# A two-block transformer on one core: query projections cut into pieces between the sums of a gather, and a triangular inverse with 64-column stationaries

## The reference, cut to what matters

```python
def peer(h, w_pq, sub_keys, expert_u, expert_v):       # 2 blocks of 128 tokens
    q = (xb @ w_pq).reshape(128, 8, 2, 128)            # w_pq 1024 x 2048
    s = jnp.einsum('thpd,hpkd->thpk', q, sub_keys)     # scores against 128 keys, twice
    sv, si = lax.top_k(s, 16)
    ...
    best, pos = lax.top_k(cand, 16)                    # 16 experts for each of 8 heads
    g = jax.nn.softmax(best, axis=-1)
    act = jax.nn.gelu(jnp.einsum('thkd,td->thk', expert_u[eidx], xb))
    return jnp.einsum('thk,thkd->td', g * act, expert_v[eidx])
```

```python
    A = jnp.where(strict, jnp.einsum('bhnik,bhnjk->bhnij', kb, k) * decay, 0.0)
    T = lax.linalg.triangular_solve(A + eye, eye, left_side=True, lower=True, unit_diagonal=True)
    u = jnp.einsum('bhnij,bhnjv->bhniv', T, v * beta[..., None])
```

## Time and profile before

| | |
|---|---|
| time, median of 3 (lowest, highest) | 1871.20 us (1868.68, 1879.18) |
| profiled execution, its own time | 1862.66 us |
| its span, mean granted TensorE clock | 1860.9 us, 0.915 |
| PE, DVE, ACT, POOL busy | 85%, 51%, 28%, 31% |
| DMA | 438.5 MB, 236 GB/s over the span |
| the gathers' queue | 299.86 MB |
| picks' stage | about 250 to 1001 us |
| inverse | about 1146 to 1172 and 1566 to 1593 us |

### The profile page before, as it was taken

How to read it: one execution, slowest core, us unless ns; L and a number is a source line. 1 busy time by engine, 2 the same in 40 slices (tenths; PEclk the granted TensorE clock), 3 DMA queues, 4 the chain that set the end, 5 groups by cost and what they waited for, 6 DMA issues and landing times.

```text
span 1860.9 us, 18421 instructions
## 1 busy us (share of the span) xinstructions
PE 1572.5 (85%) x5974; PEld 966.6 (52%) x5974; DVE 955.0 (51%) x2207; ACT 527.7 (28%) x1470; POOL 580.8 (31%) x596
## 2 busy tenths in 40 slices
PE   7998988886758667546646999999999999999998
PEld 2644654343434223212212587677775587677775
DVE  1786666756666666678876346421123246421122
ACT  2244323432223324222322254321112244321111
POOL 0010056655565767677764002100000002100000
PEclk9999999987878788767767999999999999999999
DMA  9864089988897999999999532175442422175410
GB/s 364 317 237 176 1 330 360 364 321 316 328 373 285 379 347 379 354 374 400 398 366 402 180 112 70 49 251 166 158 147 99 150 101 81 39 250 174 159 46 23
DMA packets 170725, 438.50 MB, mean 236 GB/s; under 512 B 12531, under 2 KB 59027, under 8 KB 170500
## 3 DMA queue, kind: packets, MB, share of 16 engines
q0 software_dynamic: 81824, 299.86, 42.7%
q1 hardware_dynamic: 88806, 137.46, 21.2%
HBM read 436.23 MB, written 1.05 MB: 235 GB/s over the span
## 4 chain that ended last, share of the span: by engine, by line
PE 64%; issue 11%; DVE 8%; POOL 8%; ACT 2%; DMA 2%; DVEq 2%; another core or an unknown queue 1%; SPq 0%; ACTq 0%; POOLq 0%
PE psum L1192 15%; PE psum L1203 6%; PE psum L836 5%; PE psum L966 4%; PE psum L837 4%; POOL arena L1339 4%; POOL arena L1334 4%; PE psum L668 4%; DVE arena L2296 3%; PE psum L874 2%; PE psum L1217 2%; PE psum L1180 2%; PE psum L648 2%; PE psum L850 1%; PE psum L992 1%
## 5 line engine op out<-in xcount | busy, mean ns | idle before, releaser
L836 PE MATMUL psum<-arena 128*128 128x512 f32 x382 | 249.5, 740 | 204.7 <-issue 106.6
L2296 DVE CUSTOM_DVE_ANT_0 arena<-arena,psum 128x1024 f32<-128x1024 f32 x224 | 273.6, 1221 | 185.8 <-DMA arena<-in_expert_u,indices 117.8
L1339 POOL DMA_INDIRECT arena<-in_expert_v,indices x256 | 252.8, 988 | 163.0 <-issue 71.8
L1334 POOL DMA_INDIRECT arena<-in_expert_u,indices x256 | 250.6, 979 | 92.8 <-issue 71.2
L1192 PE MATMUL psum<-activations_T,weight_ring 128*128 128x256 f32 x1280 | 279.2, 379 | 0.0
L1192 PEld LDWEIGHTS psum<-activations_T,weight_ring 128*128 128x128 f32 x1280 | 243.0, 190 | 39.8 <-issue 7.6
L836 PEld LDWEIGHTS psum<-arena 128*128 128x128 f32 x382 | 76.9, 226 | 337.3 <-issue 207.3
L2538 DVE SCALAR_TENSOR_TENSOR arena<-psum,small,arena 128x254 f32<-128x254 f32 (+1 forms) x176 | 76.8, 478 | 321.1 <-ACT arena L1797 317.5
L837 PE MATMUL psum<-arena 128*128 128x512 f32 x382 | 231.7, 693 | 0.0
L1288 POOL TENSOR_TENSOR small<-small 128x1 f32<-128x1 f32 (+5 forms) x30 | 30.7, 1024 | 532.6 <-DVE small L2432 194.4
L1614 ACT ACTIVATE activations_T<-activations_T 128x1 f32<-128x1 f32 x256 | 51.1, 200 | 348.0 <-DVE activations_T L2296 185.0
(11 more groups left out here) (408 smaller groups left out, 2052.3 us busy)
## 6 DMA issues: line engine op xcount, KB each, us to landing
weight_ring<-in_ffn_w_in SPq DMA_DIRECT2D x44, 1024.0 KB, 7.8
weight_ring<-in_w_in SPq DMA_DIRECT2D x14, 2048.0 KB, 8.4
arena<-in_ffn_w_out POOLq DMA_DIRECT2D x22, 1024.0 KB, 5.3
weight_ring<-in_w_ada SPq DMA_DIRECT2D x8, 2048.0 KB, 11.5
weight_ring<-in_w_out SPq DMA_DIRECT2D x6, 2048.0 KB, 8.5
weight_ring<-in_w_ada SPq DMA_DIRECT2D x16, 512.0 KB, 9.5
weight_ring<-in_w_pq SPq DMA_DIRECT2D x4, 2048.0 KB, 19.3
weight_ring<-in_w_in SPq DMA_DIRECT2D x2, 2080.0 KB, 21.7
```

The lines of the kernel that those rows point to most:

```text
L836: mm(o0, DIAG[:, j % ND, :], VROWS[n % NV][:, 0:512], start=m == 0, stop=last)
L1334: nc.gpsimd.indirect_dma_start(UROWS[g % NU], None, a["expert_u"], bass.IndirectOffsetOnAxis(ap=where, axis=0)).then_inc(sem(f"u_row{g % N ...
L1339: nc.gpsimd.indirect_dma_start(VROWS[g % NV], None, a["expert_v"], bass.IndirectOffsetOnAxis(ap=where, axis=0)).then_inc(sem(f"v_row{g % N ...
L2296: ttr(out=DOTJ[n >= UNIT], in0=UROWS[n % NU], in1=h2, scale=1.0, scalar=0.0, op0=ALU.mult, op1=ALU.add, accum_out=DOT[:, i, m:m + 1]).then ...
```

## The change

`queries` becomes a generator that pauses after every four matmuls (8 passes). The table runs one piece ahead of each of eight successive picks: block (0,2) before picks 13 to 20, (0,3) before 35 to 42, (1,0), (1,1), (1,2) before 53 to 60, 69 to 76, 85 to 92; (1,3) goes by two pieces before picks 101 to 104; (0,1) stays whole at pick 1. Scores, adds and the other engines' order in this stage stay.

In the inverse L1068 and L1080 take a stationary of 64 columns for each of the two sides, whose outputs go to partitions 0 to 63 and 64 to 127, and a moving operand of 64 columns; TW becomes 64 wide, its copies 256 columns, and VectorE subtracts the two diagonal blocks by an instruction each.

```diff
@@ -263,7 +263,8 @@
         RTMP = v(C0 + 2048, 2, 512)
         TI = v(C0, 8, P)
         TU = v(C0 + 1024, 8, P)
-        TW = v(C0 + 2048, 8, P)
+        TW = v(C0 + 2048, 8, 64)
+        SIDES = [slice(0, 64), slice(64, P)]
         QKT2 = v(C0 + 3072, 2, 4, SEQ)
         MO1 = v(0, 2, D, of=XT)
         AM = v(C0 + 3072, 2, 8, P)
@@ -666,10 +667,14 @@
                 for f in range(4):
                     for k in range(KT):
                         ins = mm(o[:, f * P:(f + 1) * P], wpq[b][:, k, f * P:(f + 1) * P], H2T[i][:, k, :], start=k == 0, stop=k == KT - 1)
-                ins.then_inc(a_full, 1)
-                if i == 1:
-                    was_read("a", 3 - b)
-                at["pqt"][i, b] = c["a"]
+                        if k == 3:
+                            yield
+                    if f == 3:
+                        ins.then_inc(a_full, 1)
+                        if i == 1:
+                            was_read("a", 3 - b)
+                        at["pqt"][i, b] = c["a"]
+                    yield
 
             def first_queries(hh):
                 if hh == 0:
@@ -784,11 +789,13 @@
             output(outputs[0], 1, 0, 4, KT).then_inc(d_full, 1)
             output(outputs[1], 1, 1, 4, KT).then_inc(d_full, 3)
             last_read[ON_PE[at["wout"] + 1]] = ("d", at["out1"])
-            coming = {1: lambda: queries(0, 1), 6: lambda: scores(0, 1), 20: lambda: queries(0, 2), 27: lambda: scores(0, 2),
-                      34: lambda: h2_turned(1), 42: lambda: queries(0, 3), 50: lambda: scores(0, 3),
+            coming = {6: lambda: scores(0, 1), 27: lambda: scores(0, 2), 34: lambda: h2_turned(1), 50: lambda: scores(0, 3),
                       PICKS - 12: lambda: h2_back(1, bank_a, a_full)}
+            for i, b, last, count in [(0, 1, 1, 1), (0, 2, 20, 8), (0, 3, 42, 8)] + [(1, b, QAT[b], 8 if b < 3 else 4) for b in range(4)]:
+                pieces = queries(i, b)
+                for n in range(last - count + 1, last + 1):
+                    coming[n] = lambda pieces=pieces, count=count: [next(pieces) for _ in range(8 // count)]
             for b in range(4):
-                coming[QAT[b]] = lambda b=b: queries(1, b)
                 coming[QAT[b] + 8] = lambda b=b: scores(1, b)
 
             def transposed(m, i, count):
@@ -1065,7 +1072,8 @@
                         if lv == 6:
                             ins = mm(o[64:P, h * 64:(h + 1) * 64], AT[0:64, half, h, 64:P], TI[0:64, n, 0:64], start=True, stop=True)
                             continue
-                        ins = mm(o[:, h * P:(h + 1) * P], AM[:, lv % 2, n, :], TI[:, n, :], start=True, stop=True)
+                        for side in SIDES:
+                            ins = mm(o[side, h * 64:(h + 1) * 64], AM[:, lv % 2, n, side], TI[:, n, side], start=True, stop=True)
                     ins.then_inc(a_full, 1)
                     tw[half] = c["a"]
 
@@ -1077,7 +1085,8 @@
                         o = bank_d()
                         for h in range(DH):
                             n = half * 4 + h
-                            ins = mm(o[:, h * P:(h + 1) * P], TU[:, n, :], TW[:, n, :], start=True, stop=True)
+                            for side in SIDES:
+                                ins = mm(o[side, h * 64:(h + 1) * 64], TU[:, n, side], TW[:, n, :], start=True, stop=True)
                         ins.then_inc(d_full, 1)
                         t_done[half] = c["d"]
                     m["level"].append(c["d"])
@@ -1093,7 +1102,7 @@
                     o = bank_d()
                     for h in range(DH):
                         n = half * 4 + h
-                        ins = mm(o[0:64, h * 64:(h + 1) * 64], TW[64:P, n, 0:64], TU[64:P, n, 64:P], start=True, stop=True)
+                        ins = mm(o[0:64, h * 64:(h + 1) * 64], TW[64:P, n, :], TU[64:P, n, 64:P], start=True, stop=True)
                     ins.then_inc(d_full, 1)
 
                 pe.wait_ge(d_free, c["d"])
@@ -1730,21 +1739,22 @@
                     o = full()
                     act.copy(BROWS[:, i, :, :], o.rearrange("p (h j) -> p h j", h=4)).then_inc(a_free, 1)
                 af(Z2[:, :, :], Z2[:, :, :], ACT.Silu).then_inc(sem("z_silu"), 1)
-                def heads_of(T, half):
+
+                def heads_of(T, half, width):
 
                     o = full()
-                    act.copy(T[:, 4 * half:4 * half + 4, :], o.rearrange("p (h j) -> p h j", h=4)).then_inc(a_free, 1)
+                    act.copy(T[:, 4 * half:4 * half + 4, :], o[:, 0:4 * width].rearrange("p (h j) -> p h j", h=4)).then_inc(a_free, 1)
 
                 for half in range(2):
-                    heads_of(TW, half)
+                    heads_of(TW, half, 64)
                 for lv in range(1, 6):
                     for half in range(2):
-                        heads_of(TU, half)
+                        heads_of(TU, half, P)
                         if lv < 5:
-                            heads_of(TW, half)
+                            heads_of(TW, half, 64)
                         else:
                             o = full()
-                            act.copy(TW[64:P, 4 * half:4 * half + 4, 0:64], o[64:P, 0:256].rearrange("p (h j) -> p h j", h=4)).then_inc(a_free, 1)
+                            act.copy(TW[64:P, 4 * half:4 * half + 4, :], o[64:P, 0:256].rearrange("p (h j) -> p h j", h=4)).then_inc(a_free, 1)
                 for i in range(2):
                     o = full()
                     squares([(v(C0 + 3072 + (4 * i + h) * P, P), o[:, h * P:(h + 1) * P], i * 4 + h) for h in range(DH)])
@@ -2476,7 +2486,10 @@
                             continue
                         o = full()
                         if lv < 6:
-                            tt(TI[:, s, :], TI[:, s, :], o.rearrange("p (h j) -> p h j", h=4), ALU.subtract).then_inc(d_free, 1)
+                            for side in SIDES:
+                                diagonal = TI[side, s, side]
+                                ins = tt(diagonal, diagonal, o[side, 0:256].rearrange("p (h j) -> p h j", h=4), ALU.subtract)
+                            ins.then_inc(d_free, 1)
                         else:
                             corner = TU[0:64, s, 64:P]
                             tt(corner, corner, o[0:64, 0:256].rearrange("p (h j) -> p h j", h=4), ALU.subtract).then_inc(d_free, 1)
```

## The result

| | before | changed |
|---|---|---|
| median of 4 runs (lowest, highest) | 1872.72 us (1868.68, 1879.18) | 1846.20 us (1838.72, 1850.80) |
| profiled execution, its span | 1862.66, 1860.9 us | 1838.72, 1836.9 us |
| first projection behind the gather begins at | 1019.0 us | 999.4 us |

The ratio is 0.9867, with a 95% interval of 0.9835 to 0.9899: 25 us less, where the forecast was 28. That held in the run groups in which the kernel before takes 1865 to 1873 us. The record names the chip of each later group: those with 1865 ran on two chips (5 and 8), both groups with 1775 and 1776 on a third (3). Whether the chip itself makes the difference is not shown: these are three chips, and the hour changed with them.

The account below looks back on a forecast made before the run. The gather stage was taken as bound by its gathers, with time lost where TensorE's starved query blocks delay sums. -22 and -6 make -28: 1834.7 us profiled, 1843 as median, range 1823 to 1868.

Parts of the forecast that it names:

- -22 for the pieces: Gather stage: query blocks split ahead of picks' sums remove most GpSimd waits; -22 us, at best -38.1.
- -6 for the inverse: Inverse: two column groups side by side cut a level from 4.55 to 3.7 us; -6 us, bounds -9 and +6.
- The waits go: Gather stage: GpSimd's five waits for picks' sums, 38.1 us in all, shrink to 0 to 5 us each.
- The pace behind them: Stretch of the five blocks: without waits, 3.18 us a pick falls to the later stretch's 2.81, worth 28.9 us.
- The model with one stock and one rate: TensorE in the windows: prefetched instructions plus steady supply; (0,3) and (1,1) dry up, about 7 us of 28.9 left.
- cease to arrive: TensorE in query blocks: instructions stop coming after 44 to 46 passes while gathers saturate the DMA; (1,0) takes 23.0 us.
- the one that I had put second: Dried-up windows: a sum stands within 8 passes, not at the block's end; waits of 4 to 5 us, not 8 to 9.
- There the stage is bound by the gathers: Gather stage from 640.8 us on, no query blocks: 2.81 us a pick, read as the DMA's limit.
- The multiply: Inverse: L2469, 2.64 us on VectorE between two subtractions, stops being wholly covered; 0.4 us a layer.
- The rival of serial groups: Inverse: column groups run one after another, a level takes 5.2 us, +5 in eight; 1854 us, chance 0.12.
- cold windows: TensorE's windows stay at the lower clock level, waits of 7 us remain, only the inverse gains; 1862 to 1866, chance 0.15.
- slower: Gather stage: missing instructions now hit the sums too, +35 us less 6; about 1900 us, chance 0.11.

Follow-up runs that it names:

- pieces_only: The changed kernel with the old inverse, so only the query blocks in pieces of 8 passes: 1843.75 us, ratio 0.9873 to the kernel before.
- half_rows: The kernel before, whole blocks, with most gathers fetching 2 KB a row instead of 4: 1872.4 us in a single run.
- groups_in_turn: The changed kernel with the inverse's matmuls four of one column group, then four of the other, instead of alternating: level 4.56 us against 3.90 alternating.
- pieces_doubled: The changed kernel with each of seven query blocks computed twice, in pieces of 16 passes ((0,1) whole, 32 for (1,3)): 1861.9 us in a single run.
- gpsimd_stops: The kernel before, whole blocks, with GpSimd waiting ahead of the gathers of five picks until a block is computed: ratio 1.0057 in both groups.

## Why the prediction was right, and where it was not

The forecast, 1843 for 1846.2 in the groups in which the kernel before takes 1865 us and more, rests on two terms, and both have the right sign and roughly the size: -22 for the pieces (19.6 in the traces, 21.4 of it in the stretch of the five blocks; 21.5 to 24 by pieces_only), -6 for the inverse (4.4 in the traces; 2.4, not resolved, by the times).

Point by point:
- **The waits go.** Right, and more than forecast: I kept some 7 us of waits at (0,3), (1,1) and (1,3); next to nothing was left.
- **The pace behind them.** Mis-sized. I let the stretch come down to 2.81 us a pick; it came to 228.1 / 78.5 = 2.91. What took the waits' place was not the DMA (share 0.96, and half_rows shows that the bytes don't matter here) but GpSimd's own "remote" pauses and the dots. The two errors cancel (the stretch was to be 227.5 us and is 228.1): that the sum came out is partly luck.
- **The supply of instructions.** The model with one stock and one rate failed. It said that (1,0) and (1,2) would not dry up and that (1,1) would; (1,0) and (1,2) did, for 10 us and 5 us, and (1,1) hardly, for 3 us at its end. That instructions "cease to arrive" while the gathers saturate the DMA was a reading that half_rows contradicts for the DMA and that no run shows for the instructions. The waits stayed away for another reason, the one that I had put second: a sum stands within a few passes.
- **"There the stage is bound by the gathers"** was wrong as the reading of a DMA share of 0.98 and 378 GB/s in that condition: half the bytes, same time. What remains is GpSimd's issuing, about 1.25 us a gather, two a pick, with its pauses; that it is the bound is argued from these rows, not tested.
- **The inverse.** The halves are 0.49 us, as forecast (0.48). The level is 3.89, not 3.7: I took three changes of shape at 0.13, but the chain pays about 0.15 on each of four (L1097 takes 0.66 and 0.59, L1076 0.62). The multiply costs 0.30 a layer (0.4 forecast). The rival of serial groups is out, though groups_in_turn shows that it is one loop order away.
- **The rivals "cold windows" and "slower"** did not come: no wait of 7 us is left at the split blocks, and the granted clock rose from 0.81 to 0.85 in the stretch. The mechanism of "slower", a spell that reaches a sum, exists all the same: pieces_doubled has it at (1,3).
- **A small slip.** Block (0,2) of the kernel before was said to be followed by no wait; it has one of 1.62 us at 331.01. It changes nothing in the sum.

## What to carry to other kernels

A ring of buffers covers a certain delay (14 us here), so what counts is the longest stretch in front of one release, as long as the work fits the pace: 16 passes ahead of each sum gave the whole gain, 32 less than half, 64 none, at either place. That holds where the passes dry up; where 64 passes take their 7 to 8 us, splitting gave nothing. Column groups ran side by side here only where their matmuls alternate. And a gain that lives on "issue" gaps may belong to one chip or one condition of it: time the kernel before again in each group of runs, and on another chip, before believing it.

## What was not expected of the hardware

- The same kernel took 1865 to 1873 us in some groups of runs and 1775 to 1776 in others, which ran on another chip. Up to the first projection behind the gather, the kernel before needs 1019.0 us, with the stops (gpsimd_stops, in the faster condition) 940.6; behind it 841.9 and 841.8. The first gather begins at 242.8 and 242.2. The whole difference lies in the stage in which GpSimd issues 512 gathers.
- TensorE's dry spells are not, in the main, waits for a packet of the instruction queues: in 35 of 48 none is under way.
- In the slower condition halving the gathered bytes changed neither the time nor TensorE's dry spells. In these, weight loads and matmuls arrive 0.70, 1.40 or 2.1 us apart, in steps of 0.7.
- TensorE's passes with 64 stationary columns, in two alternating groups: 16 in 0.49 us, 31 ns each; in turn 16 in 0.90, 56 ns each.
